# Far keys ahead of the rotation product, forget gates behind the attention scaling, and the linear output's sum of squares ahead of its copy, in VectorE's tail of each head

## The reference, cut to what matters

```python
z = h @ w_in[l]                      # q_h, f_fw, f_bw, i_h, g_h, q_d, k_d, v_d, gates
a = hgrn2_mixer(q_h, f_fw, f_bw, i_h, g_h, lb[l], hgrn_gnorm[l])
b = diff_attention(q_d, k_d, v_d, diff_lambda[l], lambda_init, diff_subln[l], cos, sin)
m = jax.nn.sigmoid(gate_a) * (a @ w_branch_a[l]) + jax.nn.sigmoid(gate_b) * (b @ w_branch_b[l])
```

## Time and profile before

| | us |
|---|---|
| median of 3 runs | 2473.77 |
| lowest to highest | 2473.47 to 2474.88 |
| the profiled execution, its own time | 2470.46 |
| its span, first to last instruction | 2468.5 |
| TensorE busy | 2451.6 (99%) |
| VectorE busy | 1830.1 (74%) |
| ScalarE busy | 1281.3 (52%) |
| GpSimd busy | 185.3 (8%) |
| mean granted TensorE clock | 0.999 of full speed |

### The profile page before, as it was taken

How to read it: one execution, slowest core, us unless ns; L and a number is a source line. 1 busy time by engine, 2 the same in 40 slices (tenths; PEclk the granted TensorE clock), 3 DMA queues, 4 the chain that set the end, 5 groups by cost and what they waited for, 6 DMA issues and landing times.

```text
span 2468.5 us, 41237 instructions
## 1 busy us (share of the span) xinstructions
PE 2451.6 (99%) x16634; PEld 2262.7 (92%) x16634; DVE 1830.1 (74%) x2427; ACT 1281.3 (52%) x1970; POOL 185.3 (8%) x236
## 2 busy tenths in 40 slices
PE   9999999999999999999999999999999999999998
PEld 9999989898899999888899998898889999998887
DVE  6656777754788999978575567776648888999784
ACT  4444666543355555556444456664424555564563
POOL 0001011100200000003100011011002000000031
PEclk9999999999999999999999999999999999999999
DMA  5354434254322233834233544343543232347421
GB/s 171 124 187 133 142 131 144 88 179 161 103 71 88 75 102 110 307 102 138 96 119 127 173 150 138 123 133 115 179 145 101 69 92 82 95 149 261 149 99 60
DMA packets 290267, 321.53 MB, mean 130 GB/s; under 512 B 10400, under 2 KB 223904, under 8 KB 290080
## 3 DMA queue, kind: packets, MB, share of 16 engines
q1 hardware_dynamic: 215744, 171.39, 22.5%
q10 hardware_dynamic: 74336, 147.53, 16.5%
HBM read 253.60 MB, written 65.27 MB: 129 GB/s over the span
## 4 chain that ended last, share of the span: by engine, by line
PE 92%; DVE 3%; ACT 2%; issue 1%; DMA 1%; POOL 1%; SPq 0%; ACTq 0%; POOLq 0%; DVEq 0%
PE ps L853 21%; PE ps L1140 14%; PE ps L1321 13%; PE ps L1076 9%; PE ps L811 6%; PE ps L1059 5%; PE ps L1427 5%; PE ps L1261 3%; PE ps L825 3%; PE ps L1287 2%; PE ps L1029 2%; PE ps L1407 1%; PE ps L911 1%; PE ps L1048 1%; PE ps L1009 1%
## 5 line engine op out<-in xcount | busy, mean ns | idle before, releaser
L853 PE MATMUL ps<-hT_hi,whi 128*128 128x384 f32 x608 | 204.1, 336 | 1.0 <-ACT U L2964 0.6
L853 PE MATMUL ps<-hT_lo,whi 128*128 128x384 f32 x608 | 203.1, 334 | 0.0
L853 PE MATMUL ps<-hT_hi,wlo 128*128 128x384 f32 x608 | 203.1, 334 | 0.0
L2007 DVE TENSOR_TENSOR wlo<-raw,whi 128x1024 fp32r<-128x1024 f32 (+1 forms) x154 | 165.4, 1074 | 41.9 <-ACT whi L2949 41.9
L2964 ACT ACTIVATE U<-ps 128x384 f32<-128x384 f32 x152 | 74.7, 492 | 218.4 <-PE ps L853 218.4
L1321 PE MATMUL ps<-whi,PH_hi 128*128 128x512 f32 x456 | 179.0, 393 | 0.0
L1321 PE MATMUL ps<-whi,PH_lo 128*128 128x512 f32 x456 | 177.7, 390 | 0.0
L1321 PE MATMUL ps<-wlo,PH_hi 128*128 128x512 f32 x456 | 177.5, 389 | 0.0
L1505 DVE TENSOR_TENSOR wlo<-raw,whi 128x2048 fp32r<-128x2048 f32 x53 | 122.3, 2307 | 68.1 <-ACT whi L2328 68.0
L1609 DVE TENSOR_TENSOR wlo<-raw,whi 128x1024 fp32r<-128x1024 f32 (+1 forms) x98 | 102.8, 1069 | 77.2 <-ACT whi L2490 77.1
L853 PE MATMUL ps<-S_hi,whi 128*128 128x384 f32 x456 | 152.5, 334 | 0.0
(11 more groups left out here) (318 smaller groups left out, 7039.7 us busy)
## 6 DMA issues: line engine op xcount, KB each, us to landing
raw<-w_up_dram SPq DMA_DIRECT2D x88, 512.0 KB
raw<-w_in_dram SPq DMA_DIRECT2D x64, 512.0 KB
raw<-w_down_dram SPq DMA_DIRECT2D x60, 512.0 KB, 4.6
raw<-w_in_dram SPq DMA_DIRECT2D x16, 1024.0 KB
zT<-gst ACTq DMA_DIRECT2D x40, 384.0 KB, 2.4
GT<-zT ACTq DMA_DIRECT2D x16, 768.0 KB, 5.8
pD<-CG ACTq DMA_DIRECT2D x26, 384.0 KB, 2.3
zT<-hn ACTq DMA_DIRECT2D x48, 192.0 KB, 1.8
```

Source lines behind the costliest of these rows:

```text
L853: ins = mm(ps[:, 4 * (j % 2) + bank, 0:TH], quarter(L, W[y], j, (w,))[:, 0, k * P:(k + 1) * P], sum_operand(a, x, k), start=(opens and k = ...
L2007: v.tensor_tensor(quarter(L, wlo, j, names), raw_quarter(j, names), quarter(L, whi, j, names).bitcast(F32), ALU.subtract)\
```

## The change

It moves three things in VectorE's order. The far keys and queries go ahead of the rotation product `sqk`. The forget gates of the next head go from before the wait for GpSimd's reciprocal root to behind the scaling `on`. The sum of squares of the linear output goes ahead of its copy, and the list of steps with it. No instruction is added, removed or altered.

```diff
@@ gla_names
-    out = ["o", "ss", "on", "ab0", "ab1"]
+    out = ["ss", "o", "on", "ab0", "ab1"]
@@ gla_output
                 done(G_sq, it, "sq")
+                v.tensor_reduce(st_g[:, 0, :], SQ1[:], AX_X, ALU.add).then_inc(*G_out.step("ss"))
                 v.tensor_copy(O1[:], view(ps[:], GB[0] * 512, [[P, NT], [1, P]])).then_inc(*G_out.step("o"))
-                v.tensor_reduce(st_g[:, 0, :], SQ1[:], AX_X, ALU.add).then_inc(*G_out.step("ss"))
@@ mixers, VectorE's tail
                 v.tensor_reduce(st_t[:, 0, :], SQ2, AX_X, ALU.add).then_inc(*A_dve.step("ss"))
+                far_up(it)
                 if following:
                     att_rope(it + 1, L, "sqk")
-                far_up(it)
-                if following:
-                    gla_forget(it + 1)
                 done(A_pool, it, "rs")
                 v.tensor_tensor(O2[:], O2[:], view(st_t[:], 2 * NT, [[1, NT], [0, P]]), ALU.mult).then_inc(*A_dve.step("on"))
                 if following:
+                    gla_forget(it + 1)
                     gla_keys(it + 1)
                     att_rope(it + 1, L, "radd")
                 gla_output(it)
```

## The result

The changed kernel took 2476.47 us (median of 20 runs, 2473.01 to 2478.35), the kernel before beside it on the same chip 2473.07 us. One of its 20 runs took 5007.66 us, twice the others, and is not in the ratio. The ratio is 1.0015 with a 95% interval of 1.0008 to 1.0021, so +3.7 us (between 2.0 and 5.2): slower, by less than the 0.2% that the prediction counts as a change. The prediction had +4.1 us and 2477.8 us. The profiled execution took 2474.42 us with a span of 2472.5, 4.0 us over that of before.

A forecast was written before the change was run, and what follows sets the result against it. TensorE, busy 99% of the span, was taken to bound the kernel. The terms +4.4 - 0.8 + 0.45 = +4.1 us on the median of 2473.77 gave 2477.8 us, range 2475.0 to 2481.3.

The forecast's parts named there:

- The swap: Sum ahead of copy in six tails: the diagonal stands 0.73 us for the copy in each, 4.4 us in all.
- 0.85 as the spacing: In a tail, the copy starts 0.85 us after the sum that now precedes it.
- 0.05 as TensorE's notice: The diagonal on TensorE starts 0.05 us after the copy's end.
- The second head of layer 0: Its tail: GpSimd's power gets in, far products and scaling lose their waits, linear output comes earlier: -0.8 us.
- The second head of layer 1: Its tail: the mean starts 1.42 us behind its sum, the power misses its place: +0.45 us.
- The term of 0.45: Layer 1's second head: `radd` 1.3 us later less 0.85 us of room, so sum, copy and diagonal 0.45 us late.
- The exclusive lock: SBUF port pair: by the skill, whoever starts first fully blocks the other; the trace agreed for GpSimd, not for VectorE.
- Caught in both second heads: Rival: scaling starts at 368.6 in both tails, +5.3, 2479.1 us; chance 0.25 together with the form in all six tails.
- Both gain: Rival: both second-head tails gain 0.8 us, +2.8 in all, 2476.6 us; chance 0.28.
- The swap free: Rival: something behind the diagonal was late anyway, only the gains are left, -1.6, 2472.2 us; chance 0.07.
- `radd` ends behind the square: Sign in the tails: `radd` ending after ScalarE's square in more than one tail would make the forecast wrong.

The follow-up runs named there:

- two single-part kernels: The changed kernel with the copy put back ahead of the sum of squares, 2471.48 us; the kernel before with only the sum put ahead of the copy, 2477.06 us.
- the first experiment: The changed kernel with the copy put back ahead of the sum of squares, far pair and gates left moved: 2471.48 us, ratio 0.9998 to the kernel before.
- the extra operation: The changed kernel with one more small GpSimd instruction ahead of the attention mean: 2477.13 us, ratio 1.0022.
- the last two kernels: Changed kernel, copy first, second heads' rotation products behind the far pair: 2471.55 us; with their query product behind the linear output's scaling too: 2468.49 us.

## Why the prediction was right, and where its numbers were off

**The swap (predicted 4.4).** Right in mechanism and number of tails: the diagonal waits for the copy six times. The step that was a little short is its size for one tail. It took 0.85 as the spacing and 0.05 as TensorE's notice, from the far queries. Measured are 0.86, and 0.15 from the copy's end (376.82 + 0.95 = 377.77) to the diagonal (377.92). That makes 0.83 us from linear output to diagonal in the first head instead of 0.73: 5.0 over six tails. The two single-part kernels put it at 4.2 and 4.7. Of this, 0.15 comes back behind the diagonal in each tail (3.54 to 3.39 us from diagonal to the next transposes), which the prediction had at 0. In the first and third heads the projection behind it gives it away again: it waits for ScalarE's copies (L1076 in the waits), 0.24 us in three of them, and 0.55 in layer 1's third head, where it was 0.20 before.

**The second head of layer 0 (predicted -0.8 before the swap).** Right, row by row: the power got in, the far products lost 0.52 and the linear output came at 2.67. From near products to diagonal the tail took 13.64 us against 13.51, +0.13; predicted was 0.73 - 0.8 = -0.07. Half of the difference is the swap's size again. The other half is that the kernel before had only 6.64 from linear output to diagonal in this head, where the first has 6.72, so that the front gave 0.7 and not 0.8. The 0.15 behind the diagonal covers the rest, so that the head as a whole lost 0.01. The load was early in this profile (2.99 us of wait against 3.94), but the gain does not hang on it: in the first experiment's trace, with a wait of 5.48, the transposes still follow the far products by 1.73.

**The second head of layer 1 (predicted +0.45 beside the swap).** Right in what happens, a mean that starts 1.42 behind its sum and a power that misses the place. The power was done 1.17 behind the rotation product; the prediction had 1.2. The head lost 1.29 with the swap; predicted was 0.73 + 0.45 = 1.18. That the two are so close is luck. The term of 0.45 was too large: behind a caught power the copy came only 0.17 late in the first experiment's trace, since `radd` is 1.11 later there (10.52 us behind the near products, 9.41 before) and not 1.3, and had 0.94 of room (from its own spacing of 1.67 to the copy) and not 0.85. What filled the gap is the load, which the prediction did not count: VectorE was 0.52 later against TensorE than in the profile before. To the diagonal, 0.83 + 0.17 + 0.52 = 1.52, and the table has 14.65 - 13.15 = 1.50. The lateness also explains the place of the loss: 0.50 already at the transposes, which the prediction had starting where they did. Why the mean starts 1.42 behind its sum in this head and 1.13 in layer 0, in the trace before and after alike, stays open.

**Who holds whom.** GpSimd's power was in flight from 365.42 to 366.98, and VectorE's far queries and rotation product followed each other at 0.34 and 0.35 as elsewhere. The power itself waited out the rotation product when it came 0.21 to 0.22 after its start (2.70 us), but got in within the far pair, at a cost of 0.05 to 0.24. The exclusive lock of the Trainium skill, page "SBUF — State Buffer", section "SBUF: two separate sides", is borne out for GpSimd and not for VectorE: by it the power of layer 0's second head would have held the rotation product until 366.98, and no trace here shows VectorE held: the rotation product takes 1.74 to 1.76 us in all of them, with the power in flight or without. The rows do not tell when within its 1.56 us the power reads.

**The rivals.** Caught in both second heads: not so, once in two, and it was close. In layer 0's second head the power came 0.64 ahead of the rotation product in the changed kernel's trace, but with the late load of the first experiment's only 0.11 ahead (366.96 against 367.07), and the extra operation, with the power some 0.3 later, made it miss. In layer 1's it missed by 0.21 to 0.23 in each of the five traces with the far pair first and the load in the way, and got in, 0.11 or 0.12 ahead (1.38 us), in the last two kernels, where VectorE did not wait for the load. Both gain: not so. The swap free: excluded by both single-part kernels. The sum over the heads was 4.85 us and the runs differ by 3.7, on either side of 4.1; a term too small, a term too large and a load that was not counted are in that agreement, and the run to run scatter is larger than any of them. That `radd` ends behind the square happened in one tail, as allowed.

## What to carry to other kernels

Before an instruction is moved back by one place, look at who takes the result of the one that it displaces, and at that one's room and not at its waits: the diagonal waited for nothing and had 0.17 us. With TensorE 99% busy, six stands of 0.8 us outweighed all that VectorE's better order gave here, 0.7 us in one tail. A stand that can't be avoided may be covered by exchanging two instructions of the waiting engine, as the scores and the diagonal here. And when an engine is late because of a load, push what needs the load behind what doesn't, then look where that lateness comes out next: it took a second move, of the query product, before the first one was worth anything that could be measured. And a trace is one execution: before a head's time is compared between two of them, look whether the load landed at the same place in both.

## What the runs showed of the hardware

- In these traces GpSimd's power on 128x6 takes 1.32 us alone and waits for the one two-input product of VectorE that runs when it starts, not for those behind it. What it adds is what is left of that product less 0.13 to 0.15: with 0.38 left of the far keys (365.42 of 365.80) it took 0.24 more, with 1.53 left of the rotation product (1590.47 of 1592.00) 1.38 more. The other powers of the nine traces read fit, from 0.18 left and 0.05 more upwards, except where the gates follow.
- Once in flight it is held by VectorE's TENSOR_SCALAR on 128x768, which starts 0.46 us behind it (366.81 and 367.27): 1.75 us with the gates behind the far pair, ending 0.03 to 0.04 after them, and 1.37 with VectorE idle there. A two-input product that starts 0.11 behind it (367.07 against 366.96) does not hold it: 1.37.
- TensorE's notice of VectorE's end was 0.05 us for the far products (before) and 0.15 for the diagonal (after). Why they differ was not tried.
